# Input stage of a two-layer transformer trunk: x and the first weights loaded in halves

## The reference

```python
h = rms_norm(x, attn_norm[0])
q_lat, c_kv, q_idx, k_idx, w_idx = split(h @ w_in)      # 2048, 128, 512, 64, 8 columns
dots  = einsum('bqjd,bsd->bqjs', q_idx, k_idx) * 64 ** -0.5
score = einsum('bqj,bqjs->bqs', w_idx, relu(dots))      # causal, then the top 128 keys
bias  = rel_bias[rel_bucket(t - s)]                     # one table for both attention layers
```

## Time and profile before

| | us |
|---|---|
| median of 3 runs (1227.66 to 1229.34) | 1229.24 |
| the profiled execution | 1229.2 |
| its span (first to last instruction) | 1227.4 |
| PE busy in the span | 1174.9 |
| PE busy in the first 50 us | 34.25 |

### The profile page before, as it was taken

The page is one execution under the profiler, slowest core; times in us unless marked ns, Lnnn a source line. Parts: engine busy times, 40 slices in busy tenths (PEclk is TensorE's granted clock), DMA queues, the critical chain, the costliest instruction groups (busy, mean ns, idle before and its releaser), DMA issues.

```text
span 1227.4 us, 16258 instructions
## 1 busy us (share of the span) xinstructions
PE 1174.9 (96%) x5600; PEld 968.2 (79%) x5600; DVE 594.4 (48%) x1031; ACT 464.5 (38%) x857; POOL 581.4 (47%) x319
## 2 busy tenths in 40 slices
PE   5999999999999999999999989899999999999996
PEld 4767888878888888888888778778888888888885
DVE  5479866654644444442222479855544444431111
ACT  4262346654333222323222467634322233322222
POOL 4344846675454444544445464215444455444441
PEclk8999999999999999999999989899999999999998
DMA  5831401113233333223332542112333323323331
GB/s 166 238 101 34 155 21 50 37 50 104 71 102 101 103 103 98 82 78 89 94 94 82 146 111 53 36 31 81 96 103 103 95 82 96 92 73 94 92 94 69
DMA packets 178468, 110.42 MB, mean 90 GB/s; under 512 B 7180, under 2 KB 173127, under 8 KB 178424
## 3 DMA queue, kind: packets, MB, share of 16 engines
q1 hardware_dynamic: 177984, 108.69, 31.1%
q10 hardware_dynamic: 440, 1.17, 0.3%
HBM read 107.70 MB, written 6.33 MB: 93 GB/s over the span
## 4 chain that ended last, share of the span: by engine, by line
PE 79%; DVE 8%; POOL 5%; issue 3%; DMA 2%; ACT 2%; SPq 0%; DVEq 0%; ACTq 0%; POOLq 0%
PE ps L547 25%; PE ps L549 25%; PE ps L548 25%; POOL prob L495 2%; POOL w_lo L440 2%; PE ps L753 1%; DMA b_toep<-bias_toep 1%; DVE work L1420 1%; DMA x_tok<-in_x 1%; DVE b_prob L1658 1%; DVE ss L1362 1%; PE ps L556 1%; DVE xs_lo L1349 1%; DVE work L1404 1%; DVE bpt_lo L1305 1%
## 5 line engine op out<-in xcount | busy, mean ns | idle before, releaser
L440 POOL TENSOR_TENSOR w_lo<-raw,w_hi 128x1024 fp32r<-128x1024 f32 (+1 forms) x200 | 463.0, 2336 | 509.4 <-ACT w_hi L967 500.3
L547 PE MATMUL ps<-xs_hi,w_hi 128*128 128x512 f32 (+3 forms) x1024 | 400.4, 391 | 7.9 <-DVE x L1345 3.6
L549 PE MATMUL ps<-xs_hi,w_lo 128*128 128x512 f32 (+3 forms) x1024 | 395.2, 386 | 0.0
L548 PE MATMUL ps<-xs_lo,w_hi 128*128 128x512 f32 (+3 forms) x1024 | 395.1, 386 | 0.0
L967 ACT CAST w_hi<-raw 128x1024 fp32r<-128x1024 f32 (+1 forms) x196 | 178.9, 962 | 432.9 <-PE ps L549 418.5
L547 PEld LDWEIGHTS ps<-xs_hi,w_hi 128*128 128x128 f32 x1024 | 192.8, 188 | 52.2 <-DVE x L1345 3.8
L548 PEld LDWEIGHTS ps<-xs_lo,w_hi 128*128 128x128 f32 x1024 | 192.9, 188 | 38.7 <-issue 1.1
L549 PEld LDWEIGHTS ps<-xs_hi,w_lo 128*128 128x128 f32 x1024 | 192.8, 188 | 38.7
L547 PE MATMUL ps<-act_hi,w_hi 128*128 128x512 f32 x352 | 139.2, 396 | 0.0
L549 PE MATMUL ps<-act_hi,w_lo 128*128 128x512 f32 x352 | 138.0, 392 | 0.0
L548 PE MATMUL ps<-act_lo,w_hi 128*128 128x512 f32 x352 | 136.6, 388 | 0.0
(11 more groups left out here) (186 smaller groups left out, 1402.5 us busy)
## 6 DMA issues: line engine op xcount, KB each, us to landing
raw<-in_ffn_w_gate_up SPq DMA_DIRECT2D x88, 512.0 KB, 4.7
raw<-in_ffn_w_down SPq DMA_DIRECT2D x32, 384.0 KB, 3.6
raw<-in_a_w_in SPq DMA_DIRECT2D x21, 512.0 KB, 4.8
raw<-in_ffn_w_down SPq DMA_DIRECT2D x32, 320.0 KB, 4.0
raw<-in_b_w_in SPq DMA_DIRECT2D x10, 512.0 KB, 5.0
bias_toep<-bias_row SPq DMA_DIRECT2D x1, 4096.0 KB, 21.9
toep<-bias_toep SPq DMA_DIRECT2D x16, 256.0 KB, 2.6
raw<-in_a_w_out SPq DMA_DIRECT2D x8, 512.0 KB, 4.5
```

The costliest lines, as they stand in the source:

```text
L440: nc.gpsimd.tensor_tensor(pieces(w_lo, n)[half], pieces(raw, n)[half], pieces(w_hi, n)[half].bitcast(F32), ALU.subtract)\
L547: nc.tensor.matmul(dst, wh, xh, start=start, stop=False, **kw)
L548: nc.tensor.matmul(dst, wh, xl, start=False, stop=False, **kw)
L549: return nc.tensor.matmul(dst, wl, xh, start=False, stop=stop, **kw)
```

## The change

The input stage is cut in two, "fore" and "rear", by features 0 to 511 and 512 to 1023.

- **Loads.** SP first loads the identity alone (64 KB, semaphore id_in). Then come the fore half of two x blocks, the fore half of slab 0 (semaphore raw_fore), the rear halves of both, the other tables, and slab 1. ACT loads the parameter rows first and then the fore and rear halves of the other two x blocks. The bytes are the same.
- **Transposes.** The eight tiles go to eight banks of PSUM, so none waits for a copy. PE does 16 (`x_turn(0)`), then k = 0 and 1 of slab 0 (12 matmuls), then the other 16 (`x_turn(1)`), then k = 2 to 7.
- **Parts of x.** ACT makes xs_hi, and DVE xs_lo, straight from PSUM. DVE's copy to x comes behind its xs_lo. The second half of w_hi of slab 0 moves behind tile 5 on ACT (it was behind tile 3).
- **POOL.** Three causal subtractions on `work` move from ahead of the split of slab 0 to behind it.
- **g.** Its four matmuls move on PE from ahead of `first_tiles` to behind it, into the same banks. The two copies to g_sb move on DVE from ahead of the eight additions of squares to behind them. SP's part is unchanged.

```diff
-            for t in (0, 2):
-                sp.dma_start(x_tok[:, t, :], x_in[0, t * P:(t + 1) * P, :]).then_inc(x_in_s, 16)
-            sp.dma_start(tab[:, :], consts[:, 0:C_HOT]).then_inc(tab_in, 16)
+            sp.dma_start(tab[:, 0:P], consts[:, 0:P]).then_inc(id_in, 16)
+            x_part(0)
+            raw_part(0, raw_fore)
+            x_part(1)
+            raw_part(1, raw_full[0])
+            sp.dma_start(tab[:, P:C_HOT], consts[:, P:C_HOT]).then_inc(tab_in, 16)
             slab(1, 0, wide(a_w_in[0], A_QI))
...
             for n in range(S_A2 + 2):
                 split_lo(n)
+                if n == 0:
+                    pool.wait_ge(tab_in, TAB)
+                    pool.wait_ge(set_up, 5)
+                    for i in range(1, NB):
+                        d = OFF[i] - P + i * P
+                        nc.gpsimd.tensor_tensor(work[:, d:d + P], work[:, d:d + P], causal, ALU.subtract)\
+                            .then_inc(acc_zero, 1)
...
-            pe.wait_ge(x_new, 6)
-            first_tiles((ps[:, 0, :], ps[:, 1, :]), 0, 0)
+            x_turn(0)
+            pe.wait_ge(x_new, 2)
+            first_tiles((ps[:, 0, :], ps[:, 1, :]), 0, 0, range(0, 2))
+            pe.wait_ge(par_done, 1)
+            x_turn(1)
+            first_tiles((ps[:, 0, :], ps[:, 1, :]), 0, 0, range(2, DM))
...
             for m in range(DM):
-                act.wait_ge(x_new, m + 1)
-                nc.scalar.activation(xs_hi_m(m), x[:, m, :], ACT.Copy,
+                act.wait_ge(x_tr, m + 1)
+                nc.scalar.activation(xs_hi_m(m), ps[:, m, :], ACT.Copy,
                                      scale=params[:, GAIN[0] + m:GAIN[0] + m + 1]).then_inc(xhi_done, 1)
-                if m in (1, 3):
-                    split_half(0, m // 2)
+                if m in (1, 5):
+                    split_half(0, m // 4)
...
-            dve.wait_ge(g_mm, 2)
-            nc.vector.tensor_copy(g_sb[:, 0:T], ps[0:H, 5, :]).then_inc(g_done, 1)
-            nc.vector.tensor_copy(g_sb[:, T:GLEN], ps[0:H, 4, 0:GLEN - T]).then_inc(g_done, 1)
             dve.wait_ge(set_up, 3)
             for m in range(DM):
...
                 nc.vector.tensor_tensor(ss[:, :], ss[:, :], sq_first[:, m, :], ALU.add).then_inc(ss_done, 1)
+            dve.wait_ge(g_mm, 2)
+            nc.vector.tensor_copy(g_sb[:, 0:T], ps[0:H, 5, :]).then_inc(g_done, 1)
+            nc.vector.tensor_copy(g_sb[:, T:GLEN], ps[0:H, 4, 0:GLEN - T]).then_inc(g_done, 1)
```

More of the change, by code:

```diff
@@ L231, in trunk @@
         unit_done = sem("unit_done")
-        tab_in, x_in_s, small_in, sink_in = sem("tab_in"), sem("x_in"), sem("small_in"), sem("sink_in")
+        id_in, tab_in, small_in, sink_in = sem("id_in"), sem("tab_in"), sem("small_in"), sem("sink_in")
+        x_in_s = [sem("x_in_fore"), sem("x_in_rear")]
+        raw_fore = sem("raw_fore")
         hot_in = sem("hot_in")
@@ L344, in feed_forward, with x_part, raw_part @@
                         slab(s_d + c, m, down(w_down[layer], c, m))
-            for t in (0, 2):
-                sp.dma_start(x_tok[:, t, :], x_in[0, t * P:(t + 1) * P, :]).then_inc(x_in_s, 16)
-            sp.dma_start(tab[:, :], consts[:, 0:C_HOT]).then_inc(tab_in, 16)
             r0 = raw[:, 0, :].rearrange("p (k n) -> p k n", k=DM)
             aw = a_w_in[0].rearrange("(k p) n -> p k n", p=P)
-            sp.dma_start(r0[:, :, 0:DH + JI], aw[:, :, A_KI:A_KI + DH + JI]).then_inc(raw_full[0], 16)
-            sp.dma_start(r0[:, :, P:2 * P], aw[:, :, A_CKV:A_CKV + R]).then_inc(raw_full[0], 16)
+            def x_part(half):
+                c = slice(half * T, (half + 1) * T)
+                for t in (0, 2):
+                    sp.dma_start(x_tok[:, t, c], x_in[0, t * P:(t + 1) * P, c]).then_inc(x_in_s[half], 16)
+            def raw_part(half, done):
+                k = slice(half * DM // 2, (half + 1) * DM // 2)
+                sp.dma_start(r0[:, k, 0:DH + JI], aw[:, k, A_KI:A_KI + DH + JI]).then_inc(done, 16)
+                sp.dma_start(r0[:, k, P:2 * P], aw[:, k, A_CKV:A_CKV + R]).then_inc(done, 16)
+            sp.dma_start(tab[:, 0:P], consts[:, 0:P]).then_inc(id_in, 16)
[4 more added lines that the diff above has]
+            sp.dma_start(tab[:, P:C_HOT], consts[:, P:C_HOT]).then_inc(tab_in, 16)
             slab(1, 0, wide(a_w_in[0], A_QI))
@@ L569, in tile, with first_tiles @@
                 last.then_inc(unit_done, 1)
-            def first_tiles(dst, n, e):
-                for k in range(DM):
+            def first_tiles(dst, n, e, ks=range(DM)):
+                for k in ks:
                     if k in (0, CUT_WIDE[0] // 256):
@@ L595, in norm_sum, with x_turn @@
                 nc.tensor.matmul(ps[:, 6, :], ones[:, :], ss[:, :], start=True, stop=True).then_inc(ss_sum, 1)
-            pe.wait_ge(tab_in, TAB)
+            def x_turn(half):
+                pe.wait_ge(x_in_s[half], 16 * NB)
+                for m in range(half * DM // 2, (half + 1) * DM // 2):
+                    for t in range(NB):
+                        last = nc.tensor.transpose(ps[:, m, t * P:(t + 1) * P],
+                                                   x_tok[:, t, m * P:(m + 1) * P], ident)
+                    last.then_inc(x_tr, 1)
+            pe.wait_ge(id_in, 16)
             pe.wait_ge(small_in, 16)
             nc.tensor.transpose(ps[:, 7, 0:59], par_rows[:, :], ident[0:59, 0:59]).then_inc(par_t, 1)
[L601 to L610, removed]
+            x_turn(0)
[4 more added lines that the diff above has]
+            first_tiles((ps[:, 0, :], ps[:, 1, :]), 0, 0, range(2, DM))
             pe.wait_ge(hot_in, 32)
             pe.wait_ge(rel_one, 1)
+            pe.wait_ge(x_new, DM)
             nc.tensor.matmul(ps[0:H, 5, :], rel_sb[:, :], hot[:, 0:T], start=True, stop=True).then_inc(g_mm, 1)
             nc.tensor.matmul(ps[0:H, 4, 0:GLEN - T], rel_sb[:, :], hot[:, T:GLEN], start=True, stop=True).then_inc(g_mm, 1)
-            pe.wait_ge(x_new, 6)
-            first_tiles((ps[:, 0, :], ps[:, 1, :]), 0, 0)
             pe.wait_ge(set_up, 3)
@@ L623, in _ @@
             pe.wait_ge(kw_done, 2)
+            pe.wait_ge(tab_in, TAB)
+            pe.wait_ge(g_done, 2)
             nc.tensor.matmul(ps[:, 4, :], dup, kw[0:DH, :], start=True, stop=True).then_inc(ki_dup, 1)
@@ L960, in split_half @@
             def split_half(n, half, it=0, after=0):
-                if half == 0:
+                if half == 0 and n == 0:
+                    act.wait_ge(raw_fore, 32)
+                elif half == 0 or n == 0:
                     act.wait_ge(raw_full[n % 2], 32 * (n // 2 + 1) + 32 * it)
@@ L1001, in load_table @@
                 nc.scalar.activation(spare[:, 0:1], eps[:, :], func)
[L1003 to L1006, removed]
+            act.dma_start(par_rows[:, :], par_in).then_inc(small_in, 16)
+            for half in range(2):
+                c = slice(half * T, (half + 1) * T)
+                for t in (1, 3):
+                    act.dma_start(x_tok[:, t, c], x_in[0, t * P:(t + 1) * P, c]).then_inc(x_in_s[half], 16)
             act.dma_start(hot[:, :], consts[0:BUCKETS + 1, C_HOT:C_END]).then_inc(hot_in, 16)
@@ L1068, in _ @@
             nc.scalar.copy(uv_hi[:, :, :], uv_raw[:, :, :]).then_inc(uvh_done, 1)
-            act.wait_ge(tab_in, TAB)
+            act.wait_ge(id_in, 16)
             nc.scalar.copy(ident_r[:, :], ident).then_inc(id_done, 1)
@@ L1339, in _ @@
             dve.wait_ge(par_done, 1)
[L1341 to L1352, removed]
-            dve.wait_ge(g_mm, 2)
-            nc.vector.tensor_copy(g_sb[:, 0:T], ps[0:H, 5, :]).then_inc(g_done, 1)
-            nc.vector.tensor_copy(g_sb[:, T:GLEN], ps[0:H, 4, 0:GLEN - T]).then_inc(g_done, 1)
+            for m in range(DM):
+                dve.wait_ge(xhi_done, m + 1)
+                nc.vector.scalar_tensor_tensor(xs_lo[:, m * T:(m + 1) * T], ps[:, m, :],
+                                               params[:, GAIN[0] + m:GAIN[0] + m + 1],
+                                               xs_hi[:, m * T:(m + 1) * T].bitcast(F32),
+                                               ALU.mult, ALU.subtract).then_inc(xlo_done, 1)
+                nc.vector.tensor_copy(x[:, m, :], ps[:, m, :]).then_inc(x_new, 1)
             dve.wait_ge(set_up, 3)
```

1 line of the change is left out of this document (added).

## The result

| | us |
|---|---|
| before, median | 1229.29 |
| changed kernel, median of 4 runs (1239.87 to 1241.3) | 1240.57 |
| ratio, 95% interval | 1.0091 (1.0073 to 1.0108) |
| profiled execution: span | 1238.1 (before 1227.4) |

The changed kernel is slower by 11.3 us, inside the range and 2.0 us above the forecast of 1238.6.

The account below looks back on a forecast made before the run. PE, busy 96% of the span, bounds the kernel, so only gaps count. Late g stalls PE 7.4 us, the fallen clock adds 2.0: +9.4 on 1229.2 gives 1238.6 us, range 1235 to 1242 (0.80).

Parts of the forecast that it names:

- What decides: SP's queue: g moves behind the additions, delaying slab 3; any g_sb completion above 28.4 us costs time, 7.4 us forecast.
- G: Time when g_sb is complete in the changed kernel: forecast 35.8 us, bounds 34 to 38.
- the chain from g_sb to PE's start: From g_sb through slab 3's load and POOL's low part to PE's index scores: carried over as a rigid 32.76 us.
- the choice between two answers: End of the eight additions: 35.5 us, or 34.8 if the first addition starts ahead of POOL; they differ by 0.7.
- the sum: The forecast's total: 7.4 us of PE stall plus 2.0 us of clock, +9.4 us on 1229.2.
- an estimate of 0.6 us: Loads of x's fore half: at the skill page's rate for small transfers, fore half and forecast come some 0.6 us later.
- The clock: Behind PE's stall ahead of the index scores the clock falls, costing 2.0 us; bounds 0 and 3.3.
- What hid: Edits priced at nothing, such as slab 2 landing later at about 41.3 us, hidden by 4 us of cover.
- Front end kept: Rival: slab 3 in time, so the input stage's gain counts; 1229.4 us, or 1225.4 without the clock's fall; chance 0.08.
- the wait behind 12 matmuls: Rear transposes queue on PE behind 12 matmuls of 2.7 to 4.9 us; ACT, DVE and POOL wait behind them.

Follow-up runs that it names:

- Whole loads: Changed kernel with g made early and all 32 transposes ahead of slab 0's matmuls, but x and slab 0 loaded whole: 1224.13 us, 0.9955.
- g early: Changed kernel with g's matmuls right behind the first 16 transposes and its copies behind tile 3 of x: 1231.25 us, 1.0006.
- all transposes first: Changed kernel with g made early and the second 16 transposes ahead of k = 0 and 1 of slab 0: 1223.17 us, 0.9947.
- g late: Changed kernel with only the second 16 transposes moved ahead of k = 0 and 1, g staying behind the additions: 1233.54 us, 1.0028.
- slabs ahead: Changed kernel with SP issuing slabs 2 and 3 ahead of its wait for g: 1231.58 us, 1.0015.
- slab 3 ahead: Changed kernel, g early, all 32 transposes first, additions ahead of slab 1's second half, plus slab 3 issued ahead of SP's wait for g: 1223.70 us, 0.9952.

## Why the prediction was right

**What decides.** Right, in its place and nearly in its size. G was forecast at 35.8 us and was 36.81; the chain from g_sb to PE's start at 32.76 and was 33.08. The scores were forecast to move by 7.4 us and moved by 69.89 - 61.20 = 8.69.

**Where G was mis-sized by 1.0 us.** POOL started slab 1 at 25.50 us instead of 25.0, the additions ended at 36.03 and not 34.8, and the copies cost 0.8 instead of the 1.0 between 34.8 and 35.8 (the prediction's own term for them is 0.9, so its G should read 35.7): 0.5 + 0.7 - 0.2. The 0.7 is the choice between two answers. The additions ended 5.33 us behind POOL's end, as in the kernel before (5.32). The rule of "SBUF — State Buffer" in the Trainium skill, section "Who interferes with whom", is that the first to issue holds the ports, and the sum had let one addition slip ahead by it. The rule agrees with the trace, but the order did not come out so: POOL was first by 0.01 us, and the first addition took 2.95 us, where the six behind POOL's end took 0.69 each.

**The 0.5 ahead of it** is a sum of terms of both signs. The first transpose came at 7.33 us (forecast 6.5): +0.8. From there to the first cast it took 3.1 us (2.8), from the cast to k = 0 3.6 (3.5), and the 12 matmuls 18.99 - 14.05 = 4.94 (4.9, the slow end). From the rear block to the end of slab 0's second cast it took 20.78 + 1.04 - 18.99 = 2.8 us (3.5), since the rear transposes took 1.91 us and not 3.1. From there to slab 1 on POOL it took 25.50 - 21.82 = 3.7 us (3.8):

```profile
20.78 1.04 ACT L993 CAST w_hi<-raw 128x1024 fp32r<-128x1024 f32 x1
```

```profile
21.90 2.39 POOL L455 TENSOR_TENSOR w_lo<-raw,w_hi 128x1024 fp32r<-128x1024 f32 x1 [7.96 <-ACT w_hi L993]
```

Slab 1's own cast began at 22.87 us (22.5) and was not what POOL waited for. The first term, +0.8, is the loads. The DMA engines moved 393 GB/s between 3 and 4 us in the kernel before and 180 in the changed one, whose stretches read:

```profile
3.00:4.00 1.00, 0.00 (x0) 0.00 (x0) 0.00 (x0) 0.00 (x0) 0.00 (x0) 1.00 0.65 180
4.00:5.00 1.00, 0.33 (x1) 0.18 (x1) 0.22 (x1) 0.34 (x1) 0.00 (x0) 1.00 0.95 252
5.00:6.00 1.00, 0.00 (x0) 0.00 (x0) 0.00 (x0) 0.99 (x2) 0.00 (x0) 1.00 1.06 395
```

On this side the prediction had cited the Trainium skill against the cut ("DMA: Bandwidth & Descriptors", section "Bandwidth"), with an estimate of 0.6 us from its figure, which the page gives for DMAs that GpSimd issues. The trace has 0.8. The kernel of "Whole loads" tells two causes apart: it too has the small identity and parameter loads first, but x in pieces of 512 KB, and the engines moved 319 and 410 GB/s in the same stretches:

```profile
3.00:4.00 1.00, 0.00 (x0) 0.00 (x0) 0.00 (x0) 0.30 (x1) 0.00 (x0) 1.00 0.85 319
4.00:5.00 1.00, 0.33 (x1) 0.18 (x1) 0.17 (x1) 0.99 (x2) 0.00 (x0) 1.00 1.01 410
```

So in the two stretches the small loads ahead go with 74 and 8 GB/s less than in the kernel before, and the smaller pieces with another 139 and 158.

**The clock: right in kind, too large, and in the total by luck.** Forecast 2.0 us for the fall behind the stall. The spans differ by 10.7 us and the scores' start by 8.7, which leaves 2.0. But the fall at the stall accounts for 1.5 of it only: the second group of scores is 73.50 - 63.33 = 10.2 us late. The sum took over the 4.50 us at half clock from a gap of 3.56 us. Here the clock had fallen from about 66.4 us on, while PE was idle, and only 3.51 us of work stood behind the stall before it was back. The rest is a sum that nobody forecast. At 120.00 us the kernel before has a wait of PE for POOL of 2.16 us, and the changed kernel has the same one, 2.17 us, at 130.09. The clock stayed up behind it before and fell in the changed kernel:

```profile
120.00:124.90 4.90, 4.90 (x21) 4.05 (x22) 4.90 (x15) 2.14 (x3) 4.90 (x4) 1.00 0.24 60
```

```profile
130.10:135.00 4.90, 4.90 (x14) 3.87 (x15) 4.90 (x15) 2.15 (x3) 4.90 (x4) 0.65 0.26 68
```

At the next wait of both kernels, 176.49 and 188.22 us, the distance was 11.7 us. By the end it was 10.7, since later stretches gave back 1.1.

**What hid.** Slab 2's cast did wait for its load, until 43.81 us, and nobody waited for it in turn, as the sum had it. `norm_sum` was forecast 1.2 to 1.9 us sooner and came 0.6 sooner, and its half clock took that back. "Front end kept" was forecast at 1229.4 us if the chain were no matter; with g early the kernel took 1231.25, 1.0006 of the kernel before. SP has twelve DMAs ahead of its wait, not eleven as counted ahead of the result, all issued by 10.5 us; that changes nothing.

**What it had not seen as a way out.** It named the wait behind 12 matmuls as new, but priced it only through G. It is the reason that the input stage gave nothing: without it, and with g early, the same stage is 6 us faster than before.

## What to carry to other kernels

A wait in a queue that only issues DMAs delays everything written behind it, however small what it waits for: before moving a producer, follow its semaphore into that queue and read when the loads behind it are needed. Where a late step sets the earliest start of PE, price the change by that chain alone, since work saved ahead of it only makes the wait longer, and add the clock that PE loses by waiting, of which only the part behind the wait costs anything. Small work that fills an early gap on PE is not free when other engines are fed by what is queued behind it.

## What the runs showed of the hardware

The granted clock's record and the pace of the matmuls disagreed early in the span. In the changed kernel the row of 14.05 to 18.45 us has a granted clock of 1.00 with 10 matmuls in 4.40 us, 0.44 us each, which is the pace of the 0.50 rows; the transposes took 3.67 us for the first 16 and 1.91 for the second:

```profile
7.33:11.00 3.67, 3.67 (x16) 3.27 (x16) 1.64 (x3) 1.91 (x3) 0.00 (x0) 1.00 1.11 337
14.05:18.45 4.40, 4.40 (x10) 3.48 (x11) 0.69 (x2) 0.00 (x0) 0.00 (x0) 1.00 0.47 150
18.99:20.90 1.91, 1.91 (x18) 1.91 (x17) 0.55 (x1) 1.27 (x3) 0.00 (x0) 1.00 0.00 0
```

So a clock of 1.00 before the first change of the record is no evidence of full speed; the distance between starts is. In the kernel with all transposes first the second block took 3.65 us, and with g late 1.94 us, so the moment at which PE speeds up differs between kernels that are alike up to there, and no row announces it.

The same wait can cost the clock or not. In all eleven kernels PE waits 2.1 to 2.2 us for POOL somewhere between 111 and 132 us. In the 4.90 us behind it the granted clock was 1.00, with 21 matmuls, in the kernel before and in four others (slabs ahead, all transposes first, slab 3 ahead, whole loads), and 0.65, with 14 or 15 matmuls, in the remaining six. Six or seven matmuls fewer at 0.23 us each are 1.4 to 1.6 us at one wait, as much as several of the differences compared here. What decides it no run shows, nor whether every execution of a kernel does the same.

Behind a copy of 4 MB inside HBM, the two loads of slab 3 on SP landed 14.6 to 15.7 us after their issue in the changed kernel, and after 15.6 to 16.3 before. Such a load lands in 4.6 us when it is ahead of the copy. Their issues took 4.2 and 5.1 us each; the prediction calls the queue full there, and no row shows what held them.
